# Weight sums over five groups, a pass's feature sums in the next pass, first weights a unit sooner

## The chip, the core and the metric

The kernel runs on one core of a Trainium2 chip, in one launch. The metric is the device time of an execution in microseconds. The five engines of the core run programs of their own and meet at semaphores: TensorE (PE) multiplies, VectorE (DVE) and ScalarE (ACT) work element by element, GpSimd (POOL) and SyncE (SP) here mostly issue transfers (DMAs). In the code `wait_ge` is a wait on a semaphore, `then_inc` counts one up, and `alone` is an empty instruction that carries the waits before it.

## What is computed

One layer of a hybrid encoder, in float32, for 2048 prompt rows and 64 sample rows with caches (2112 rows, model width 1024). Cut to its frame:

```python
q, k, v, z, xbc, dt, u, vc = split_cols(x @ w_in, IN_SIZES)
o_a = band_attention(q, k, v, table)
o_b = mamba_mixer(z, silu(causal_dwconv(xbc)), dt, ...)      # 4 taps
o_c = chunk_mlp(gelu(u), gelu(vc), ...)
x = layer_norm(ALPHA * x + concat(norms) @ w_out)
up = causal_dwconv(x @ ffn_w_in)                             # 3 taps, 2 x 2816 features
gate, val = split_cols(up, (2816, 2816))
x = layer_norm(ALPHA * x + (silu(gate) * val) @ ffn_w_out)
```

Each float32 product is made of three matmuls of halves (high x high, high x low, low x high), so every operand is split into a high part (a copy on ScalarE) and a low part (a subtraction on VectorE). Both projections of the feed-forward part are made with a scheme of seven products for 2 x 2 blocks in place of eight (Strassen's, in Winograd's form), which needs sums and differences of blocks of the weights and of the features.

## The kernel before

Seven stages run one after another: project_rows, project_features, attention, ssd_and_gmlp, mix_out, ffn_up, ffn_down. Within a stage each engine's program has its order written out; what runs when follows from these orders and the semaphores. The change touches project_features, ffn_up and the first waits of ffn_down.

**project_features** (`pf_`) makes queries, keys and xbc with features on partitions. Rows come in groups of 304 (g = 0 to 5, and a last one of 288), 13 units of 24 matmuls each: six of queries and keys, then seven of xbc (the last group takes xbc first). A unit's result lies in one of eight PSUM banks. For xbc unit j, ScalarE copies the bank to `cin` (L792, L790), VectorE makes the four taps into `conv` (L876 to L894), ScalarE applies silu (L779 to L782), SP stores it to xbc_t (L658); `cin`, `conv` and `conv_out` have two buffers each. Beside this VectorE makes, for the down-projection, four sums of blocks of ffn_w_out for each of 11 blocks kk (`sum_weights`, L841 to L848): SP loads 1 MB to `fdw_raw` (one buffer), VectorE sums into `fdw_sum` (one buffer), SP stores it to fd_w_sum and only then loads the next block. The sums come behind xbc units 1, 3, 5 of groups 1, 2 and 4, and behind unit 0 of groups 3 and 5. GpSimd, which loads rows for the groups, then waits for all 11 stores before it loads the attention's bias, queries and keys (L721 to L735).

**ffn_up** (`fu_`) runs three passes q over pairs of row blocks (352 rows each), in each 22 units j, one for each tile of 128 gate and 128 value features. A unit is seven products of 12 matmuls, in the order 1, 2, 6, 5, 7, 3, 4; ScalarE and VectorE combine them as c11 (L2933), c22 (L2951), c12 (L2959) and c21, and TensorE starts product 4 when c22 is taken out of its bank. Then come three taps, silu and the product h = silu(gate) * val (`products_h`, L2857, L2859). Each pair of units gives sums of h for the down-projection (`half_sums`): behind an even unit one difference (L2870), behind an odd one three sums (L2877, L2878, L2881), made between the gate's taps and c22 of the unit after. In the first pass VectorE also sums and splits the weights (L2812 to L2831), which are stored and loaded again by later passes. Values of h lie in `val0`, `val1` or an even tile's own buffer, and go to fd_h_val, fd_h_mix and fd_h_sum. At each turn to the next pass VectorE makes differences of the new features (`differences`, L2614 to L2631) in the last two units. The tensors `xb` are free during a pass, and `half_sum` and the even tiles' first buffers lie over them.

In the third pass the first weights of the down-projection come in too: SP issues four loads of 512 KB (`load_fd_w`, L2529) behind its part of unit 1, and ScalarE and VectorE split two of the pieces in unit 1 (L2775, L2886), between p5's copy and c22, and two in unit 20:

```python
if isinstance(j, int) and j == 1 and q + 1 == NQ:
    sp.wait_ge(x_lo_done, 7 * NQ)
    for piece in range(4):
        load_fd_w(piece)
```

**ffn_down** waits for all stores of h, sums and differences, and multiplies.

## Time and profile before

| what | value |
|---|---|
| time, 3 runs | median 2656.88 us, 2654.92 to 2657.43 |
| the profiled execution's own time | 2656.61 us |
| its span | 2654.8 us |
| PE busy | 2502.1 us (94%) |
| DVE busy | 1799.4 us (68%) |
| ACT busy | 1122.4 us (42%) |
| POOL busy | 199.0 us (7%) |
| moved by DMA | 528.55 MB, mean 199 GB/s |

How the rows are read. Times are microseconds from the span's start. A row of busy times by stretch has: the stretch, its length, then for PE, PEld (PE's weight loads), DVE, ACT and POOL the busy time with the count of instructions, then the granted clock of TensorE as a share of full speed, the mean busy share of the 16 DMA engines, and the GB/s that they moved. A row of a timeline has: start, duration, engine, line, operation, what it writes <- what it reads, the shapes, xcount, and in square brackets how long the engine was idle before it and what ended that; SPq is SP's queue of issues. A row of waits has: who waited <- for whom: us in total, times, longest. A landing row has the time from issue to landing, least/median/most. Matmuls overlap, so one of 0.33 us starts every 0.16.

### The profile page before, as it was taken

Reading aid. Unit: us, or ns where it says so; the run is one execution under the profiler, and the core shown is the slowest. Engines: PE = TensorE matmul, PEld = TensorE weight load, DVE = VectorE, ACT = ScalarE, POOL = GpSimd, SP = SyncE. Lnnn points to the kernel's source line nnn. Section 1 sums busy time; section 2 is a strip of 40 time slices with the busy share of each in tenths; the row PEclk is TensorE's granted clock in tenths of the full one; section 3 lists DMA queues with packets and bytes.
Section 4 is the critical chain, followed back from the end, with each engine's and each line's share of the span. In section 5 each row is a group of like instructions: output and inputs, shape, how many; then the busy total and the mean of one; then the engine's idle time right before and its main releaser. Section 6 shows DMA issues by size and latency. Waiting matters only on the chain. (4 is left out here: it accounts for less than half of the span.)

```text
span 2654.8 us, 45838 instructions
## 1 busy us (share of the span) xinstructions
PE 2502.1 (94%) x14723; PEld 2305.4 (87%) x14723; DVE 1799.4 (68%) x3398; ACT 1122.4 (42%) x2112; POOL 199.0 (7%) x271
## 2 busy tenths in 40 slices
PE   6999988997999989997999989999799999999998
PEld 5888888997999978887999979999799997888786
DVE  5433445565777777778999986667777775355787
ACT  4454412224665552325555554444455453222231
POOL 0001100010101850110000000000000000000000
PEclk9999999998999989998999999999999999999999
DMA  6446545466644654647877779888678867575564
GB/s 206 147 141 204 170 155 182 161 217 160 154 109 124 215 185 152 213 154 252 268 242 248 250 234 297 258 253 261 209 259 257 265 197 207 137 215 140 163 168 137
DMA packets 459877, 528.55 MB, mean 199 GB/s; under 512 B 67690, under 2 KB 381324, under 8 KB 458338
## 3 DMA queue, kind: packets, MB, share of 16 engines
q1 hardware_dynamic: 439356, 464.21, 56.5%
q0 software_dynamic: 19408, 62.38, 7.3%
q8 instruction: 66, 1.08, 0.2%
q10 hardware_dynamic: 998, 0.48, 0.1%
q14 instruction: 49, 0.40, 0.0%
HBM read 342.66 MB, written 187.20 MB: 200 GB/s over the span
## 5 line engine op out<-in xcount | busy, mean ns | idle before, releaser
L2994 PE MATMUL fu_banks<-mo_fu_x_hi,mo_fu_w 128*128 128x354 f32 (+1 forms) x1848 | 609.1, 330 | 58.2 <-DVE fu_c L2951 40.3
L2996 PE MATMUL fu_banks<-mo_fu_x_hi,mo_fu_w 128*128 128x354 f32 (+1 forms) x1848 | 605.6, 328 | 0.0
L2995 PE MATMUL fu_banks<-fu_x_lo_rest,mo_fu_w 128*128 128x354 f32 (+1 forms) x1584 | 518.9, 328 | 0.0
L2994 PEld LDWEIGHTS fu_banks<-mo_fu_x_hi,mo_fu_w 128*128 128x128 f32 x1848 | 353.1, 191 | 69.3 <-issue 27.7
L2996 PEld LDWEIGHTS fu_banks<-mo_fu_x_hi,mo_fu_w 128*128 128x128 f32 x1848 | 353.0, 191 | 0.0
L2995 PEld LDWEIGHTS fu_banks<-fu_x_lo_rest,mo_fu_w 128*128 128x128 f32 x1584 | 302.3, 191 | 0.0
L3302 DVE TENSOR_TENSOR fu_fd_h_a<-fu_fd_h_raw,fu_fd_h_hi 128x768 fp32r<-128x768 f32 x108 | 95.7, 890 | 156.1 <-ACT fu_fd_h_hi L3257 155.8
L3257 ACT CAST fu_fd_h_hi<-fu_fd_h_raw 128x768 fp32r<-128x768 f32 (+1 forms) x116 | 88.1, 761 | 267.5 <-DMA fu_fd_h_raw<-fd_h_sum 106.3
L127 PE MATMUL pr_ps_y<-pr_w_hi,pr_xt_hi 128*128 128x512 f32 (+3 forms) x408 | 148.5, 364 | 4.7 <-DVE pr_xt_lo L404 4.7
L128 PE MATMUL pr_ps_y<-pr_w_lo,pr_xt_hi 128*128 128x512 f32 (+3 forms) x408 | 147.5, 362 | 0.0
L129 PE MATMUL pr_ps_y<-pr_w_hi,pr_xt_lo 128*128 128x512 f32 (+3 forms) x408 | 146.9, 360 | 0.0
L2673 ACT ACTIVATE fu_gate<-fu_c,fu_vecs 128x352 f32<-128x352 f32 (+1 forms) x132 | 90.1, 682 | 73.4 <-DVE fu_c L2933 63.0
L2846 DVE SCALAR_TENSOR_TENSOR fu_gate<-fu_c,fu_vecs,fu_gate 128x352 f32<-128x352 f32 (+1 forms) x132 | 76.9, 583 | 58.1 <-ACT fu_gate L2673 58.1
L1441 PE MATMUL at_ps_o<-pf_at_v,at_pt 128*128 (+2 forms) x900 | 111.7, 269 | 0.0
L127 PE MATMUL mo_ps_y<-sg_mo_w_hi,sg_mo_mt_hi 128*128 128x512 f32 (+1 forms) x272 | 108.2, 398 | 3.4 <-PEq L1490 3.4
L1441 PEld LDWEIGHTS at_ps_o<-pf_at_v,at_pt 128*128 128x128 f32 (+1 forms) x900 | 107.9, 191 | 1.1
L128 PE MATMUL mo_ps_y<-sg_mo_w_lo,sg_mo_mt_hi 128*128 128x512 f32 (+1 forms) x272 | 106.7, 392 | 0.0
L129 PE MATMUL mo_ps_y<-sg_mo_w_hi,sg_mo_mt_lo 128*128 128x512 f32 (+1 forms) x272 | 106.6, 392 | 0.0
L127 PE MATMUL fu_banks<-fu_fd_wa,fu_fd_h_hi 128*128 128x512 f32 x256 | 101.6, 397 | 3.4 <-DVE fu_fd_h_a L3302 2.5
L2823 DVE TENSOR_TENSOR mo_fu_w<-fu_w_raw,mo_fu_w 128x1024 fp32r<-128x1024 f32 x65 | 79.5, 1223 | 32.7 <-ACT mo_fu_w L2646 32.7
L129 PE MATMUL fu_banks<-fu_fd_wa,fu_fd_h_a 128*128 128x512 f32 x256 | 100.9, 394 | 0.0
L128 PE MATMUL fu_banks<-fu_fd_wa,fu_fd_h_hi 128*128 128x512 f32 x256 | 100.9, 394 | 0.0
(462 smaller groups left out, 6001.0 us busy)
## 6 DMA issues: line engine op xcount, KB each, us to landing
mo_fu_w<-fu_w_split SPq DMA_DIRECT2D x176, 512.0 KB, 4.7
fu_w_split<-mo_fu_w SPq DMA_DIRECT2D x44, 1024.0 KB, 4.1
fu_w_raw<-ffn_w_in SPq DMA_DIRECT2D x87, 512.0 KB, 5.5
fd_h_sum<-fu_half_sum SPq DMA_DIRECT2D x22, 528.0 KB, 6.3
pf_fdw_raw<-ffn_w_out SPq DMA_DIRECT2D x11, 1024.0 KB, 7.1
fd_w_sum<-pf_fdw_sum SPq DMA_DIRECT2D x11, 1024.0 KB, 4.8
fu_w_raw<-ffn_w_in SPq DMA_DIRECT2D x44, 256.0 KB, 5.3
x_rows<-pr_xr SPq DMA_DIRECT2D x16, 512.0 KB, 2.9
```

The source lines that it names most:

```text
L127: pe.matmul(out, lhs_hi, rhs_hi, start=first, stop=False)
L128: pe.matmul(out, lhs_hi, rhs_lo, start=False, stop=False)
L129: return pe.matmul(out, lhs_lo, rhs_hi, start=False, stop=last)
L1441: last = pe.matmul(ps_o[:b.nq, par, 0:HD], pt[:w, par, k, :b.nq], vals, start=(k == 0), stop=(k == b.nb - 1))
L2673: act.activation(out, src[:, 0:n], ACT.Identity, bias=one(vecs[:, 3, :], mt), scale=one(vecs[:, 0, :], mt)).then_inc(tap0_done, 1)
L2823: dve.tensor_tensor(w_lo[:, p, W_A11:W_A12 + 1], w_raw[:, p, 0].rearrange("p (a k) c -> p a k c", a=2), w_hi[:, p, W_A11:W_A12 + 1].bitcas ...
L2846: dve.scalar_tensor_tensor(out=out, in0=src[:, 1:1 + n], scalar=one(vecs[:, 1, :], mt), in1=out, op0=ALU.mult, op1=ALU.add).then_inc(tap1_ ...
L2994: pe.matmul(out, wh, xh, start=first and k == 0, stop=False, skip_group_check=True)
L2995: pe.matmul(out, wh, xl, start=False, stop=False, skip_group_check=True)
L2996: last = pe.matmul(out, wl, xh, start=False, stop=k == KH - 1, skip_group_check=True)
L3257: act.copy(h_hi[:, n % RING, 0:raw.shape[1], 0:raw.shape[2]], raw).then_inc(h_hi_done, 1)
L3302: dve.tensor_tensor(low, raw, high.bitcast(F32), ALU.subtract).then_inc(h_lo_done, 1)
```

## The change

Three parts. **Weight sums:** `fdw_raw` holds two blocks; SP issues the first two loads; from then on ScalarE issues the store of a block's sums and the load of the block two further on, behind the silu of the xbc unit after the one that the sums follow. The sums now follow xbc units 1, 4 of groups 0, 2 and 3, units 0, 2, 4 of group 1, and units 0, 2 of group 4. Three empty instructions go, and the loop over groups is written out. **Feature sums:** in the first pass tiles 0 to 19 get no sums (`is_late`). Even and odd tiles both use `val1`, and SP stores them to fd_h_mix. In the second pass SP loads a pair of these tiles back (`load_late`, in the even unit), VectorE makes the four sums in the odd unit (`late_sums`, behind `half_sums`), SP stores them (`store_late`, at that unit's end). `late_raw` and `late_sum` lie over `xb`, so the third pass's differences wait for all late stores; the second pass's no longer wait for sums and differences of the first. **First weights:** the four loads are issued behind SP's part of unit 0 of the third pass.

```diff
--- before.py
+++ after.py
@@ -523,17 +523,13 @@
         ps_y = m.ps("ps_y", [P, 8, 512])
         assert m.here() <= HEAD_AT
-        fdw_raw, fdw_sum = m.over("fdw_raw", raw_at, [P, 2, D]), m.over("fdw_sum", raw_at + 8 * D, [P, 4, 512])
+        fdw_raw, fdw_sum = m.over("fdw_raw", raw_at, [P, 2, 2, D]), m.over("fdw_sum", raw_at + 16 * D, [P, 4, 512])
+        assert 24 * D <= 16 * W
         d["fd_w_sum"] = nc.dram_tensor("fd_w_sum", (KF // 2, P, 4 * 512), F32, kind="Internal").ap()
-        fdw_loaded, fdw_done, fdw_stored = m.sem("fdw_loaded"), m.sem("fdw_done"), m.sem("fdw_stored")
-
-        def fdw_at(g, p, i, j):
-
-            if isinstance(g, int):
-                return {1: 0, 3: 1, 5: 2}.get(j) if g == 1 else None
-            if p:
-                return 4 * i + 2 if j == 0 else None
-            return {1: 4 * i - 1, 3: 4 * i, 5: 4 * i + 1}.get(j)
+        fdw_loaded, fdw_done, fdw_stored = [m.sem("fdw_loaded0"), m.sem("fdw_loaded1")], m.sem("fdw_done"), m.sem("fdw_stored")
+
+
+        FDW = {(0, 1): 0, (0, 4): 1, (1, 0): 2, (1, 2): 3, (1, 4): 4, (2, 1): 5, (2, 4): 6, (3, 1): 7, (3, 4): 8, (4, 0): 9, (4, 2): 10}
         w_loaded = [m.sem(f"w_loaded{k}") for k in range(4)]
         w_hi_done, w_lo_done = m.sem("w_hi_done"), m.sem("w_lo_done")
...
@@ -614,6 +610,10 @@
         def xbc_count(g, j):
             return (NXBC + 1 - j % 2) // 2 * g + j // 2
+
+        def load_fdw(eng, kk):
+            rows = d["ffn_w_out"].rearrange("(k e p) c -> k p e c", e=2, p=P)[kk]
+            eng.dma_start(fdw_raw[:, kk % 2], rows).then_inc(fdw_loaded[kk % 2], 16)
         with nc.Block() as block:
             @block.sync
@@ -625,20 +625,9 @@
                     sp.dma_start(w_raw[:, k % 4, 0:2 * AW], d["w_in"][rows, 0:2 * AW]).then_inc(w_loaded[k % 4], 16)
                     sp.dma_start(w_raw[:, k % 4, 2 * AW:], d["w_in"][rows, X0:X0 + XBC]).then_inc(w_loaded[k % 4], 16)
-                def load_fdw(kk):
-                    pair = slice(kk, kk + 1) if isinstance(kk, int) else bass.ds(kk, 1)
-                    rows = d["ffn_w_out"].rearrange("(k e p) c -> k p e c", e=2, p=P)[pair]
-                    sp.dma_start(fdw_raw[:], rows.rearrange("a p e c -> p (a e) c")).then_inc(fdw_loaded, 16)
-
-                def sums_of(kk):
-
-                    sp.wait_ge(fdw_done, 4 * kk + 4)
-                    alone(sp)
-                    pair = slice(kk, kk + 1) if isinstance(kk, int) else bass.ds(kk, 1)
-                    sp.dma_start(d["fd_w_sum"][pair].rearrange("a p c -> p (a c)"), fdw_sum[:].rearrange("p s c -> p (s c)")).then_inc(fdw_stored, 16)
-
                 sp.wait_ge(w_lo_done, KD - 1)
-                load_fdw(0)
+                for kk in range(2):
+                    load_fdw(sp, kk)
                 def step(g, p, i):
                     n = width(g)
...
-                            sums_of(kk)
-                            if not (p if not isinstance(g, int) else kk == 2):
-                                load_fdw(kk + 1)
-                        if not isinstance(g, int) and p == 0 and j == 0:
-                            load_fdw(4 * i - 1)
                     if tail(g):
                         store_qk(range(AHEAD))
                         sp.wait_ge(states_done, 2)
@@ -781,6 +763,15 @@
                         else:
                             act.activation(conv_out[:, j % 2, :n], conv[:, j % 2, :n], ACT.Silu).then_inc(silu_done, 1)
+                    def behind(j):
+
+                        if (g, j - 1) in FDW:
+                            kk = FDW[g, j - 1]
+                            act.wait_ge(fdw_done, 4 * kk + 4)
+                            act.dma_start(d["fd_w_sum"][kk], fdw_sum[:].rearrange("p s c -> p (s c)")).then_inc(fdw_stored, 16)
+                            if kk + 2 < KF // 2:
+                                load_fdw(act, kk + 2)
+
                     for j in range(NXBC):
                         wait_if(act, conv_done, NXBC * g + j - (1 if j != 0 else 0) if j != 1 else NXBC * g)
                         act.wait_ge(y_done, at_unit(g, 1, j))
@@ -792,7 +783,9 @@
                             act.copy(cin[:, j % 2, 3:3 + n], y).then_inc(evac_done, 1)
                         if j >= 1:
                             silu(j - 1)
+                            behind(j - 1)
                     silu(NXBC - 1)
+                    behind(NXBC - 1)
                     if tail(g):
                         act.wait_ge(ncum_done, 2)
                         act.activation(ecum[:], ncum[:], ACT.Exp, scale=-1.0)
@@ -834,17 +827,14 @@
                 def sum_weights(kk):
-                    b11, b12, b21, b22 = (fdw_raw[:, e, c:c + 512] for e in range(2) for c in (0, 512))
-                    dve.wait_ge(fdw_loaded, 16 * kk + 16)
+                    b11, b12, b21, b22 = (fdw_raw[:, kk % 2, e, c:c + 512] for e in range(2) for c in (0, 512))
+                    dve.wait_ge(fdw_loaded[kk % 2], 16 * (kk // 2 + 1))
                     wait_if(dve, fdw_stored, 16 * kk)
-                    alone(dve)
                     dve.tensor_tensor(fdw_sum[:, 0], b12, b11, ALU.subtract).then_inc(fdw_done, 1)
                     dve.tensor_tensor(fdw_sum[:, 2], b22, b12, ALU.subtract).then_inc(fdw_done, 1)
                     dve.wait_ge(fdw_done, 4 * kk + 1)
-                    alone(dve)
                     dve.tensor_tensor(fdw_sum[:, 1], b22, fdw_sum[:, 0], ALU.subtract).then_inc(fdw_done, 1)
                     dve.wait_ge(fdw_done, 4 * kk + 3)
-                    alone(dve)
                     dve.tensor_tensor(fdw_sum[:, 3], fdw_sum[:, 1], b21, ALU.subtract).then_inc(fdw_done, 1)
                 dve.wait_ge(vec_done, 1)
...
-                            sum_weights(kk)
+                        if (g, j) in FDW:
+                            sum_weights(FDW[g, j])
                     if tail(g):
                         dve.wait_ge(cum_done, 1)
                         dve.tensor_scalar(ncum[:], ps_y[:, 6, 0:NC_ * HEADS].rearrange("p (t h) -> p t h", h=HEADS), -1.0, None,
...
@@ -2326,7 +2315,9 @@
         block_at = [head_at + 4 * KH * WX * slot for slot in range(7)]
         half_sum = m.over("half_sum", block_at[X_T4], [P, 3, 354])
-        even_first = m.over("even_first", block_at[X_T2], [P, 354]), m.over("diff_first", block_at[X_T2] + 1440, [P, 354])
+        late_raw, late_sum = m.over("late_raw", block_at[X_T2], [P, 4, 352]), m.over("late_sum", block_at[X_T3], [P, 4, 352])
+
+        LATE = KF - 2
...
@@ -2409,12 +2401,12 @@
                 return (q + 1, j + n - KF) if q + 1 < NQ else None
             return (q, j + n)
-        def evens(q, j):
-
-            return even_first if q == 0 and not (isinstance(j, int) and j >= KF - 2) else even_later
+        def is_late(q, j):
+            return q == 0 and not (isinstance(j, int) and j >= LATE)
         def second(q, j, p):
-            return val1 if p else evens(q, j)[0]
+
+            return val1 if p or is_late(q, j) else evens[0]
         def raws(q, j, p):
...
@@ -2511,8 +2503,28 @@
                     alone(sp)
                     sp.dma_start(flat(h_val[:, one_tile(j), cols]), val0[:, :n]).then_inc(h_stored[0], 16)
+                def load_late(j):
+
+                    pair = slice(j, j + 2) if isinstance(j, int) else bass.ds(j, 2)
+                    if not isinstance(j, int):
+                        sp.wait_ge(late_done, 2 * j)
+                    sp.wait_ge(h_stored[0], 16 * LATE)
+                    sp.wait_ge(h_stored[1], 16 * LATE)
+                    alone(sp)
+                    sp.dma_start(late_raw[:, 0:2], h_val[:, pair, 0:352]).then_inc(late_loaded, 16)
+                    sp.dma_start(late_raw[:, 2:4], h_mix[:, pair, 0:352]).then_inc(late_loaded, 16)
+
+                def store_late(j):
+
+                    sp.wait_ge(late_done, 2 * j + 2)
+                    alone(sp)
+                    sp.dma_start(h_sum[:, :, one_tile(j), 0:352].rearrange("p s a c -> p (s a) c"), late_sum[:, 0:3]).then_inc(late_stored, 16)
+                    sp.dma_start(flat(h_mix[:, one_tile(j - 1), 0:352]), late_sum[:, 3]).then_inc(late_stored, 16)
...
@@ -2573,6 +2585,11 @@
                             store_h(*before(q, j), 1 - p)
                         if i == (4 if q else 3) and not is_first(q, j):
                             store_sums(*before(q, j), 1 - p)
+                        if q == 1 and not (isinstance(j, int) and j >= LATE):
+                            if i == 1 and p == 0:
+                                load_late(j)
+                            if i == 6 and p:
+                                store_late(j)
                         if i == 3 and last:
                             sp.wait_ge(mm_done, 7 * (NU - 1) + 3)
...
@@ -2584,7 +2601,7 @@
                     if isinstance(j, int) and j == 1 and q + 1 < NQ:
                         sp.wait_ge(x_lo_done, 7 * (q + 1))
                         load_x(q + 1)
-                    if isinstance(j, int) and j == 1 and q + 1 == NQ:
+                    if isinstance(j, int) and j == 0 and q + 1 == NQ:
                         sp.wait_ge(x_lo_done, 7 * NQ)
...
@@ -2609,6 +2626,8 @@
                     eng.wait_ge(xb_loaded[1], loaded_x(q)[0])
                     eng.wait_ge(rest_loaded, loaded_x(q)[1])
                     eng.wait_ge(xb_zeroed, 2 if q == NQ - 1 else 1)
+                    if q == NQ - 1:
+                        eng.wait_ge(late_stored, 16 * LATE)
                     if q:
...
@@ -2619,15 +2638,12 @@
                 def t2_step():
                     eng.wait_ge(t_done, 4 * q + 2)
-                    if q == 1:
-
-                        eng.wait_ge(diff_stored, 16 * (KF // 2 - 1))
                     eng.tensor_tensor(t2, b22, t1, ALU.subtract).then_inc(t_done, 1)
                 def t4_step():
                     eng.wait_ge(t_done, 4 * q + 3)
-                    if q:
-                        eng.wait_ge(sums_stored, 16 * (KF // 2 * q - 1))
+                    if q == NQ - 1:
+                        eng.wait_ge(sums_stored, 16 * (KF // 2))
                     eng.tensor_tensor(t4, b21, t2, ALU.subtract).then_inc(t_done, 1)
                 return t3_step, t1_step, t2_step, t4_step
...
@@ -2742,11 +2759,14 @@
                     if turn:
                         split_x_hi(q + 1, 3)
                     act.wait_ge(add_done, 3 * u + 2)
-                    if p:
-                        wait_if(act, h_stored[1], 8 * u - 8)
-                        wait_if(act, sums_done, 2 * u - 3)
+                    v = u - LATE
+                    if is_late(q, j):
+                        wait_if(act, h_stored[1], 16 * u)
+                    elif p:
+                        act.wait_ge(h_stored[1], 16 * LATE + 8 * v - 8)
+                        wait_if(act, sums_done, 2 * v - 3)
                     else:
-                        wait_if(act, sums_done, 2 * u - 2)
+                        wait_if(act, sums_done, 2 * v - 2)
                         if q == NQ - 1:
                             wait_if(act, rest_stored, 8 * j)
                     if q == NQ - 1:
...
@@ -2879,6 +2902,22 @@
                     dve.wait_ge(sums_done, 2 * u + 1)
                     alone(dve)
                     dve.tensor_tensor(s4, val0[:, :n], s2, ALU.subtract).then_inc(sums_done, 1)
+
+                def late_sums(j):
+
+                    a11, a12, a21, a22 = (late_raw[:, i] for i in range(4))
+                    s1, s2, s4, s3 = (late_sum[:, i] for i in range(4))
+                    dve.wait_ge(late_loaded, 16 * j + 16)
+                    wait_if(dve, late_stored, 16 * j - 16)
+                    alone(dve)
+                    dve.tensor_tensor(s3, a11, a21, ALU.subtract).then_inc(late_done, 1)
+                    dve.tensor_tensor(s1, a21, a22, ALU.add).then_inc(late_done, 1)
+                    dve.wait_ge(late_done, 2 * j - 1)
+                    alone(dve)
+                    dve.tensor_tensor(s2, a22, s3, ALU.subtract).then_inc(late_done, 1)
+                    dve.wait_ge(late_done, 2 * j + 1)
+                    alone(dve)
+                    dve.tensor_tensor(s4, a12, s2, ALU.subtract).then_inc(late_done, 1)
                 def fd_w_lo(piece):
                     high, low, raw = fd_w_piece(piece)
@@ -2941,6 +2980,8 @@
                         split_lo(*nxt, 1 - p, 1)
                     if not is_first(q, j):
                         half_sums(*before(q, j), 1 - p)
+                    if q == 1 and p and not (isinstance(j, int) and j >= LATE):
+                        late_sums(j)
                     for piece in fd_w_here(q, j):
                         fd_w_lo(piece)
...
```

## Rows read from the trace of the kernel before

**Rows 1.** Busy times by stretch: project_features, then pairs and passes of ffn_up.

```profile
334.00:377.33 43.33, 43.16 (x311) 42.91 (x309) 16.88 (x40) 9.12 (x20) 4.21 (x4) 1.00 0.34 107
377.33:435.00 57.67, 48.61 (x312) 47.87 (x313) 35.12 (x86) 14.88 (x28) 0.91 (x1) 0.88 0.53 183
435.00:629.00 194.00, 178.07 (x1257) 176.66 (x1255) 111.50 (x274) 45.22 (x113) 14.93 (x23) 0.96 0.57 185
1257.46:1288.68 31.22, 29.27 (x169) 28.83 (x169) 28.28 (x47) 16.37 (x26) 0.00 (x0) 0.95 0.89 283
1319.11:1349.54 30.43, 27.84 (x168) 27.27 (x169) 28.19 (x47) 16.37 (x26) 0.00 (x0) 1.00 0.78 248
1575.79:1850.04 274.25, 273.64 (x1681) 273.00 (x1681) 192.43 (x343) 127.61 (x220) 0.00 (x0) 1.00 0.85 267
1600.00:1628.90 28.90, 28.90 (x178) 28.64 (x177) 20.28 (x37) 13.07 (x23) 0.00 (x0) 1.00 1.04 324
```

**Rows 2.** Timeline of TensorE in project_features, its two longest waits.

```profile
398.24 0.62 PE L127 MATMUL pf_ps_y<-pr_pf_xs,pr_pf_w 128*128 128x304 f32 x1 [6.66 <-ACT pf_cin L792]
...
606.83 0.61 PE L127 MATMUL pf_ps_y<-pr_pf_xs,pr_pf_w 128*128 128x288 f32 x1 [7.30 <-ACT pf_cin L790]
```

**Rows 3.** Timeline of VectorE in project_features; landing of the stores of pf_fdw_sum.

```profile
374.01 0.16 DVE L876 COPY pf_cin<-pf_halo 128x3 f32<-128x3 f32 x1
...
439.91 0.69 DVE L841 TENSOR_TENSOR pf_fdw_sum<-pf_fdw_raw 128x512 f32<-128x512 f32 x1 [6.06 <-DMA pf_fdw_raw<-ffn_w_out]
...
442.51 0.16 DVE L876 COPY pf_cin<-pf_halo 128x3 f32<-128x3 f32 x1
...
444.77 0.16 DVE L876 COPY pf_cin<-pf_halo 128x3 f32<-128x3 f32 x1
...
DMA to landing us min/median/max: 3.9/4.8/7.3
```

**Rows 4.** Timeline in project_features, one instruction of ScalarE, one of GpSimd.

```profile
605.90 0.39 ACT L779 ACTIVATE pf_conv_out<-pf_conv 128x224 f32<-128x224 f32 x1 [9.97 <-DMA xbc_t<-pf_conv_out]
...
581.32 0.83 POOL L722 DMA_DIRECT2D pf_bias<-pf_bias_rows  x1 [95.08 <-DMA fd_w_sum<-pf_fdw_sum]
```

**Rows 5.** Waits of TensorE in the first pass; timeline of VectorE there.

```profile
PE fu_banks L2994 <- DVE fu_c L2951: 23.4, 17, 2.1
...
1332.59 0.52 DVE L2870 TENSOR_TENSOR fu_diff_first<-fu_val,fu_even_first 128x352 f32<-128x352 f32 x1
...
1333.02 0.52 DVE L2951 TENSOR_TENSOR fu_c<-fu_part,fu_banks 128x354 f32<-128x354 f32 x1
...
1347.39 0.52 DVE L2877 TENSOR_TENSOR fu_half_sum<-fu_even_first,fu_val 128x352 f32<-128x352 f32 x1
...
1348.89 0.52 DVE L2951 TENSOR_TENSOR fu_c<-fu_part,fu_banks 128x354 f32<-128x354 f32 x1
```

**Rows 6.** Timeline of VectorE at the turn to the second pass.

```profile
1547.61 1.63 DVE L2631 TENSOR_TENSOR mo_fu_xb<-mo_fu_xb 128x1416 f32<-128x1416 f32 x1 [3.34 <-DMA fd_h_sum<-fu_half_sum]
```

**Rows 7.** Timelines in the later passes of ffn_up.

```profile
1697.36 0.52 DVE L2951 TENSOR_TENSOR fu_c<-fu_part,fu_banks 128x354 f32<-128x354 f32 x1 [0.65 <-PE fu_banks L2996]
...
1834.02 2.26 SPq L2545 DMA_DIRECT2D mo_fu_w<-fu_w_split  x2
...
1840.26 1.63 DVE L2614 TENSOR_TENSOR mo_fu_xb<-mo_fu_xb 128x1424 f32<-128x1424 f32 x1
...
2169.03 2.35 DVE L2886 TENSOR_TENSOR fu_fd_wa<-fu_fd_wa_raw,fu_fd_wa 128x1024 fp32r<-128x1024 f32 x2
...
2171.87 0.43 PE L2994 MATMUL fu_banks<-mo_fu_x_hi,mo_fu_w 128*128 128x356 f32 x1 [0.98 <-DVE fu_c L2951]
```

**Rows 8.** Timelines at the third pass's second unit, by start.

```profile
1899.11 2.38 SPq L2529 DMA_DIRECT2D fu_fd_wa_raw<-ffn_w_out  x4
...
1905.08 1.04 ACT L2775 CAST fu_fd_wa<-fu_fd_wa_raw 128x1024 fp32r<-128x1024 f32 x1 [9.82 <-DMA fu_fd_wa_raw<-ffn_w_out]
...
1909.24 0.66 PE L2994 MATMUL fu_banks<-mo_fu_x_hi,mo_fu_w 128*128 128x356 f32 x1 [10.59 <-DVE fu_c L2951]
```

50 lines of the change are left out of this document (27 added, 23 removed).

## The prediction

> **What bounds the kernel now.** I read the page first: TensorE is busy for 94% of the span and VectorE for 68%, averages over stages with different limits. So the busy times by stretch came second, with a stretch for each stage that the change touches; then the waits of TensorE in these stretches; then the timeline of VectorE, ScalarE and the DMA queues around each wait.
>
> In project_features a group of 13 units takes 43.33 us where TensorE never waits. The next 13 took 57.67 us with 48.61 busy and a granted clock of 0.88, and the rest of the stage 194.00 us [rows 1]. The largest waits are 6.66 us and, in the last group, 7.30 us, both for ScalarE's copies out of PSUM [rows 2]. Behind the first stands a chain: VectorE waits 6.06 us for a weight block that one buffer holds [rows 3], ScalarE waits for VectorE's convolution, TensorE for ScalarE. Behind the second, ScalarE waits 9.97 us for a store of xbc_t to land, in the stretch in which GpSimd's queue moves the attention's first tiles; GpSimd had stood 95.08 us for the last weight sums before it began [rows 4].
>
> In ffn_up's first pass a pair of units takes 30.43 us with VectorE busy for 28.19, or 31.1 to 31.2 at clock 0.95. The second pass needs 274.25 us for 20 units with TensorE busy for all but 0.6 and VectorE for 70% [rows 1]: 13.68 us a unit, 27.4 a pair. In the first pass TensorE waits for VectorE's c22 17 times, 23.4 us [rows 5]: VectorE is the bound there, TensorE in the second. At the third pass's second unit TensorE stands 10.59 us [rows 8].
>
> **Part 1, the sums of weights.** The work is the same: 11 blocks, each 2.60 us on VectorE (439.91 to 442.51), against 2.26 us for one convolution (442.51 to 444.77) [rows 3]. What goes is the wait for the block, since two are held and each is asked for two sums ahead. What comes is a wait for the sums' store before fdw_sum is written again. The store is issued by ScalarE behind the next silu and lands in 3.9 to 7.3 us, median 4.8 [rows 3]. Sums two units apart wait for it, three apart hardly.
>
> ScalarE now issues a store and a load at each sum. Nearest price: four loads issued by SP took 2.38 us, 0.6 each [rows 8], so at most 1.2 a sum. Queued behind them is the next copy into cin, and behind that VectorE and TensorE. Silu, two issues and copy need about 2.1 us, less than a convolution. I charge nothing to VectorE and count 0.8 us on each copy behind a sum. SP's queue loses both transfers, and xbc_t's stores no longer stand behind them.
>
> After group 0 the two sums there delay VectorE by 5 to 8 us. Group 1's convolutions began at 374.01 [rows 3], though the matmuls of its first xbc unit were through by 334 + 7 x 3.33 = 357.3: VectorE works through queries and keys first, which wait for their stores, and the bias rows travel at the time. These stores do not all shift, so part of the delay is absorbed. I take C = 377 (bounds 374, nothing arrives, and 380). With sums behind j = 0, 2 and 4, the copies that TensorE needs at 377.33 plus 3.33 for each unit stand at C+3.2, C+8.8, C+10.3, C+19.4 and C+21.5: C, one convolution more for each, 2.60 for a sum, and 2.3 to 3.5 for the store not yet landed. TensorE stands 2.9, 2.3, 0, 3.9 and 0 us: 9.1, against the 9.06 idle (57.67 less 48.61) of now. So these 13 units gain nothing: between 3 better at C = 374 and 3 worse at 380, the slower clock with them a little more.
>
> From group 2 on VectorE keeps up: it is busy 111.50 us of the 194 [rows 1], 28 for each group of 13 units, sums in them; even with 8 us of waits for stores that is 36, under 43.33. I expect no wait of TensorE. The rest of the stage becomes 3 x 43.33 for three groups and 41.8 for the last (288 of 304 columns, and the decay sums): 172 instead of 194 [rows 1], so 22 less. This takes the 7.30 us with it: the last sums are stored in group 4, some 50 us sooner, and the bias and the first keys travel during group 5's copies, whose banks are wanted again four units or 13.3 us later. Bounds: 27 if C stays, 10 if the tail still stands its 7.3 with its slow restart and C is late.
>
> The Trainium skill (DMA: Bandwidth & Descriptors, Issuing engines are not separate DMA queues) says that DMAs of ScalarE and SP run on the same 16 engines and that a second issuer saves issue time only. By it, landings would stay as they are, which the sum above supposes.
>
> **Part 2, the first pass's sums.** Removed from each pair: the difference (1332.59 to 1333.02, 0.43 us) and three sums (1347.39 to 1348.89, 1.50) [rows 5]. VectorE is the bound, so a pair becomes 30.43 - 1.93 = 28.5, still over TensorE's 27.4. Ten pairs: 19.3 us. Five of the ten now run about 0.7 longer at clock 0.95; with waits of 0.6 instead of 1.95 I expect clock 1.00: 3.4 more, 22.7. Floor: 27.4 a pair would give 33; ceiling: only 19. val1 now serves even tiles too, so ScalarE must wait for h_mix's store; it is issued some 5 us before (products_h, then c11, one sum and the gate's taps lie between). A store of 1 MB lands in 4.8 [rows 3]; this one has 176 KB: nothing. If it took 7, 2 us a unit would come back.
>
> At the turn to the second pass VectorE waited 3.34 us for the last store of half_sum [rows 6]; that buffer lies idle now. Gain 3.3.
>
> The second pass gets 4 more operations in each odd unit. They stand ahead of c22 and cost 1.94 us (0.43 each, and one dependence). There VectorE had come 0.65 us too soon [rows 7], so c22 moves by 1.29. How much it bears is shown at the last but one unit: 2.35 us of fd_w_lo put ahead of c22 cost TensorE 0.98 [rows 7]; slack 1.3 to 1.4. So 0 to 0.2 an odd unit: 1 us in all, bound 6 if the even unit's slack is not the odd one's. SP gets two loads and two stores a pair; ahead of load_w and of the h stores they take 1.2 us each time, behind a unit of slack.
>
> At unit 20 the differences for the third pass overwrite late_sum, and wait for the last late store. SP issues it behind load_w, from 1836.3 on (1834.02 + 2.26), two transfers, landed some 6 us later (the 4.8 of rows 3 and the issue of two), at 1842.3; VectorE wants to begin at 1840.26 [rows 7]. 2 us late, and c22, c12 and the splits of x behind it: 2 us (0 to 5).
>
> Transfers: a pair gains 704 KB of loads and as much of stores, 1.44 MB in 27.4 us, 53 GB/s on top of 267 [rows 1]: 320. The stretch at 1600 shows 324 for 28.9 us with TensorE never idle. Just hidden; load_w has a unit of slack.
>
> **Part 3, the down-projection's first weights.** The four loads go out behind unit 0's last load_w instead of unit 1's, one unit or 13.7 us sooner: 1885.4 instead of 1899.11. The first landed in 6.0 (1899.11 to 1905.08) [rows 8]: now at 1891.4, the second by 1893. ScalarE comes for them at 1895.26 (1905.08 - 9.82). SP's next load_raw waits 2.4 us behind them, two units ahead of its use. Left are two casts and two subtractions before c22, which cost 0.98 at the other such place [rows 7]; casts come first here, so 0.65. Gain 9.9, and 1.3 for the clock: the first matmul behind took 0.66 instead of 0.43 [rows 7, 8] (bounds 0 and 6, since 9.06 idle in rows 1 went with 5.3 more lost).
>
> **Sum.** 22 + 22.7 + 3.3 + 11.2 - 1 - 2 = 56.2 us. The profiled execution took 2656.61 around a span of 2654.8; less 56.2 it is 2600.4, and the median shown is 0.3 higher: 2600.7.
>
> **Rivals.**
> A: group 0's sums push group 1 behind the bias rows' traffic, C is 385 or the store lands in 7 us, so groups 1 to 3 stay late, and the tail still waits for xbc_t: part 1 gives 8. For it: the 16.7 us that the convolutions of group 1 are late already now. Against: VectorE's load is under TensorE's from group 2 on. 2615. Chance 0.20.
> B: the late sums reach TensorE in every odd unit by the whole 1.2 us, with the clock dips that rows 1 show for waits of 2 us: 12 to 15 back. For it: slack measured in an even unit only. 2613. Chance 0.15.
> C: the first pass falls to TensorE's own pace, 27.4 a pair: 10 more. Against: 28.5 counted on VectorE. 2590. Chance 0.10.
> D, slower: the second pass becomes bound by transfers. It would have to move no more than 267 GB/s in the mean: 8.77 MB at 267 is 32.8 us a pair, 5.4 x 10 = 54 back, and at 250 it is slower by 20: 2677. Against: 324 over 28.9 us. The Trainium skill (DMA: Bandwidth & Descriptors, Where 436 GB/s comes from) puts the HBM side at about 358 GB/s for a core; by that 320 still fits, with little left. Chance 0.03.
> E: the stalls have another cause than the waits I named, and nothing moves: 2657. Chance 0.02.
> The forecast has 0.50: its own range is 2592 to 2609. The whole range, 2586 to 2622, takes in A to C and leaves out D, E and the ends. A measurement here tells about 0.2%, 5 us, from no change. Faster 0.95, same 0.02, slower 0.03.
>
> **What would show it.** In the profile after: no wait of VectorE for weight blocks in project_features, one or two of 2 to 3.5 us for their store, and TensorE's waits in that stage about 9 us, all near group 2's start; pairs of 28.5 us in the first pass; 13.7 a unit and some 320 GB/s in the second; one wait of 2 us of VectorE at its unit 20; about 0.65 us instead of 10.59 at the third pass's second unit. Waits behind group 2, a second pass over 277 us for the same 20 units, or ScalarE waiting for h_mix would make it wrong.

## The result and the profile after

The changed kernel takes 2615.37 us (median of 4 runs, 2614.35 to 2618.04) against 2655.9 for the kernel before on the same chip (4 runs, 2654.37 to 2657.43): ratio 0.9849, 95% interval 0.9832 to 0.9866. That is 40.5 us faster where 56.2 were forecast. The time lies in the whole range (2586 to 2622) and outside the forecast's own (2592 to 2609). The profiled execution took 2615.82 us around a span of 2614.0, 40.8 less than the 2654.8 of before.

Four matmuls cut both traces into stages: project_features' first (287.84 before, 287.46 after), the attention's first (634.14 and 620.34), ffn_up's first (1207.36 and 1188.18) and ffn_down's first (2197.18 and 2156.65). The ledger by stage, in us, with ffn_up cut further:

| part of the span | before | after | measured | forecast |
|---|---|---|---|---|
| project_features to the attention | 346.30 | 332.88 | -13.4 | -22 |
| attention, segment sums, mix | 573.22 | 567.84 | -5.4 | 0 |
| ffn_up's first pass with its turn | 368.43 | 348.14 | -20.3 | -22.7 - 3.3 |
| second pass, 20 units | 274.25 | 284.85 | +10.6 | +3 |
| turn to the third pass | 34.67 | 34.67 | 0 | 0 |
| third pass | 287.16 | 275.43 | -11.7 | -11.2 |
| the rest (start, last unit, ffn_down) | 770.8 | 770.2 | -0.6 | 0 |

The ffn_up rows run between the matmuls that follow a c22 (before: 1575.79, 1850.04, 1884.71 and 2171.87, of which [rows 1, 7] show the ends; after: 1536.32, 1821.17, 1855.84 and 2131.27), the first from ffn_up's first matmul.

Busy times by stretch of the kernel after. The first two stretches answer to 334 to 435 and 435 to 629 in [rows 1], the third to the pair there, the fourth to its second pass:

```profile
333.62:444.20 110.58, 92.62 (x620) 90.77 (x619) 60.15 (x142) 23.14 (x48) 5.11 (x5) 0.92 0.57 193
444.20:617.28 173.08, 173.08 (x1257) 172.81 (x1255) 107.03 (x267) 44.31 (x114) 14.77 (x23) 1.00 0.54 176
1298.53:1327.08 28.55, 27.85 (x168) 27.27 (x169) 26.40 (x43) 16.37 (x26) 0.00 (x0) 1.00 0.76 246
1536.32:1821.17 284.85, 277.58 (x1681) 274.42 (x1681) 210.90 (x383) 126.66 (x220) 0.00 (x0) 0.99 0.99 305
```

The last 1257 matmuls of project_features take 173.08 us instead of 194.00, with TensorE never idle and clock 1.00, where 172 was forecast. The two groups ahead of them take 110.58 instead of 101.00: there the gain is given back. The pair of the first pass takes 28.55 (forecast 28.5). In the second pass TensorE is busy for 277.58 us, 3.9 more than the 273.64 of [rows 1], and idle for 7.3 where it was idle for 0.6; the DMA share is 0.99.

TensorE's three largest waits in project_features after, with VectorE's timeline in the same stage and the landing of the stores of pf_fdw_sum:

```profile
350.50 0.41 PE L127 MATMUL pf_ps_y<-pf_xs_slot,pr_pf_w 128*128 128x304 f32 x1 [3.19 <-ACT pf_cin L783]
...
392.77 0.59 PE L127 MATMUL pf_ps_y<-pr_pf_xs,pr_pf_w 128*128 128x304 f32 x1 [8.41 <-ACT pf_cin L783]
...
408.15 0.62 PE L127 MATMUL pf_ps_y<-pr_pf_xs,pr_pf_w 128*128 128x304 f32 x1 [2.99 <-ACT pf_cin L783]
```
```profile
349.44 0.69 DVE L833 TENSOR_TENSOR pf_fdw_sum<-pf_fdw_raw 128x512 f32<-128x512 f32 x1 [6.03 <-DMA fd_w_sum<-pf_fdw_sum]
...
389.36 0.16 DVE L866 COPY pf_cin<-pf_halo 128x3 f32<-128x3 f32 x1
```
```profile
DMA to landing us min/median/max: 3.9/5.0/10.5
```

Before its second sum of group 0 VectorE waits 6.03 us: the store of the first landed in 10.5 us, over the 7.3 that was the most before [rows 3]. Group 1's convolutions begin at 389.36 instead of 374.01 [rows 3]. TensorE pays for it already inside group 1 (3.19 us) and then at group 2 (8.41 and 2.99). Behind 409 TensorE has no wait of 0.9 us or more in this stage: the 7.30 us of [rows 2] are gone, and VectorE waits for no block load any more.

GpSimd's queue stood beside that store (timeline, and the row of DMA issues with its time to landing):

```profile
336.76 1.11 POOL L697 DMA_DIRECT2D pf_bias_rows<-rel_ext  x1 [5.97 <-PE pf_ps_y L129]
354.42 1.10 POOL L697 DMA_DIRECT2D pf_bias_rows<-rel_ext  x1 [16.55 <-PE pf_ps_y L129]
```
```profile
pf_bias_rows<-rel_ext POOLq DMA_DIRECT2D x1, 640.0 KB, 26.3
```

At ffn_up's first pass one wait is new, at the third unit. TensorE's timeline, with the regular wait of a later pair under it; ScalarE's; and SP's queue of issues:

```profile
1244.72 0.42 PE L3035 MATMUL fu_banks<-mo_fu_x_hi,mo_fu_w 128*128 128x354 f32 x1 [2.45 <-DVE mo_fu_w L2851]
...
1298.53 0.42 PE L3035 MATMUL fu_banks<-mo_fu_x_hi,mo_fu_w 128*128 128x354 f32 x1 [0.49 <-DVE fu_c L2992]
```
```profile
1241.95 0.68 ACT L2689 ACTIVATE fu_val<-fu_c,fu_vecs 128x352 f32<-128x352 f32 x1 [6.01 <-DMA fd_h_mix<-fu_val]
```
```profile
1223.40 5.38 SPq L2467 DMA_DIRECT2D mo_fu_xb<-x1t  x4
1229.22 5.00 SPq L2450 DMA_DIRECT2D fu_w_raw<-ffn_w_in  x2
1234.57 3.01 SPq L2499 DMA_DIRECT2D fd_h_mix<-fu_val  x1
```

ScalarE waits 6.01 us for the store of h_mix from the one value buffer. That store's issue alone took 3.01 us (others: 0.34 to 0.37, one 0.51), behind two loads of weights (5.00) and the four loads of the next x (5.38). The two pairs from 1236.17 to 1298.53 take 62.36 instead of 2 x 28.55: 5.3 lost, once.

In the second pass, TensorE's two waits, ScalarE's and VectorE's that lie behind them, and three of ScalarE's copies of c11's part (one a unit):

```profile
1573.35 0.43 PE L3035 MATMUL fu_banks<-mo_fu_x_hi,mo_fu_w 128*128 128x354 f32 x1 [3.61 <-ACT fu_part L2726]
...
1818.33 0.43 PE L3035 MATMUL fu_banks<-mo_fu_x_hi,mo_fu_w 128*128 128x354 f32 x1 [3.02 <-ACT fu_part L2745]
```
```profile
1572.30 0.64 ACT L2689 ACTIVATE fu_val<-fu_banks,fu_vecs 128x352 f32<-128x352 f32 x1 [7.01 <-DMA fd_h_val<-fu_val]
...
1600.55 0.46 ACT L2726 COPY fu_part<-fu_banks 128x354 f32<-128x354 f32 x1 [1.21 <-PE fu_banks L3037]
...
1614.48 0.46 ACT L2726 COPY fu_part<-fu_banks 128x354 f32<-128x354 f32 x1 [0.96 <-PE fu_banks L3037]
...
1628.13 0.46 ACT L2726 COPY fu_part<-fu_banks 128x354 f32<-128x354 f32 x1 [1.21 <-PE fu_banks L3037]
```
```profile
1811.38 1.64 DVE L2633 TENSOR_TENSOR mo_fu_xb<-mo_fu_xb 128x1424 f32<-128x1424 f32 x1 [2.81 <-DMA fd_h_mix<-fu_late_sum]
```

The copies stand 13.93 and 13.65 us apart in turn; before it was 13.65 each time. So the late sums ahead of c22 cost 0.28 us in every odd unit, 2.8 in all; it does not show as idle time, since matmuls overlap. What it is shows at one matmul behind c22, which starts 0.33 us after the one ahead of it instead of 0.16 and takes 0.42 instead of 0.33:

```profile
1609.96 0.32 PE L3037 MATMUL fu_banks<-mo_fu_x_hi,mo_fu_w 128*128 128x354 f32 x1
1610.29 0.42 PE L3035 MATMUL fu_banks<-mo_fu_x_hi,mo_fu_w 128*128 128x354 f32 x1
```

One wait of 3.61 us stands near the pass's start, behind ScalarE's 7.01 for h_val's store; one of 3.02 at its unit 20, behind VectorE's 2.81 for the last late store. These are 9.4 of the 10.6 us. Behind the first wait the granted clock falls to 0.86 in a stretch of 10 us, which is 1.4 us lost if all of it delays the matmuls, and so about the rest of 1.2; from 1590 to 1818 it is 1.00:

```profile
1575.00:1585.00 10.00, 10.00 (x55) 10.00 (x55) 7.80 (x16) 3.87 (x7) 0.00 (x0) 0.86 1.08 369
```

At the third pass's second unit, TensorE in place of the 10.59 us of [rows 8]:

```profile
1870.23 0.44 PE L3035 MATMUL fu_banks<-mo_fu_x_hi,mo_fu_w 128*128 128x356 f32 x1 [0.45 <-DVE fu_c L2992]
```

### The profile page after: what moved, and what is told of

Same layout as the page of the kernel before. It is cut to its first block and busy times, and to the rows that moved or that the text cites. A ratio compares the mean times of both kernels' runs of the same rounds, so it can differ in the third digit from the quotient of the medians.

```text
span 2614.0 us, 45349 instructions
## 1 busy us (share of the span) xinstructions
PE 2488.4 (95%) x14723; PEld 2290.0 (88%) x14723; DVE 1799.6 (69%) x3398; ACT 1118.0 (43%) x2109; POOL 199.2 (8%) x271
## 3 DMA queue, kind: packets, MB, share of 16 engines
q1 hardware_dynamic: 442204, 452.25, 56.2%
## 5 line engine op out<-in xcount | busy, mean ns | idle before, releaser
L3035 PE MATMUL fu_banks<-mo_fu_x_hi,mo_fu_w 128*128 128x354 f32 (+1 forms) x1848 | 607.0, 328 | 40.5 <-DVE fu_c L2992 12.9
L3035 PEld LDWEIGHTS fu_banks<-mo_fu_x_hi,mo_fu_w 128*128 128x128 f32 x1848 | 350.7, 190 | 54.2 <-ACT fu_part L2745 13.4
```

What stands on the lines that cost most here:

```text
L3035: pe.matmul(out, wh, xh, start=first and k == 0, stop=False, skip_group_check=True)
```

## The experiments

Every kernel was profiled and timed beside the kernel before, in five rounds (the one with more traffic in three). The stage between the attention's first matmul and ffn_up's first took 566 to 582 us in these profiles though no edit touches it, and single times of one kernel spread over up to 22 us. So effects of a few us are read from stage times in the profiles, and the ratios stand beside them. Stage times have a spread of their own, which kernels with the same program of a stage show: project_features takes 329.6 to 334.5 us in the six kernels that have it as after, and 321.7 to 325.8 in the four with the sums a group later; ffn_up takes 968.5 to 971.1 and its second pass 300.5 to 302.8 in the four that have these as after. An effect of 2 us on a stage is hardly more than that, and rests on the single waits named beside it. "Second pass" is here 21 units, from the first c22 matmul of the pass (1536.32 after) to the one with a wait of 1.1 to 1.7 us at the turn (1836.79).

| kernel | median | ratio to before (95%) | project_features | middle | ffn_up | second pass |
|---|---|---|---|---|---|---|
| before | | | 346.30 | 573.22 | 989.82 | 289.88 |
| after | 2615.37 | 0.9849 (0.9832-0.9866) | 332.88 | 567.84 | 968.47 | 300.47 |
| e1 part 1 only | 2642.66 | 0.995 (0.9931-0.9969) | 331.27 | 568.27 | 989.43 | 289.63 |
| e2 parts 2, 3 only | 2633.33 | 0.9916 (0.99-0.9932) | 344.84 | 566.87 | 970.19 | 302.10 |
| e3 sums later | 2608.82 | 0.9832 (0.981-0.9854) | 321.92 | 566.07 | 968.52 | 300.55 |
| e4 two buffers | 2623.69 | 0.9868 (0.9849-0.9888) | 332.47 | 578.42 | 966.20 | 301.08 |
| e5 loads behind | 2616.95 | 0.9856 (0.9832-0.9881) | 334.51 | 570.96 | 966.54 | 298.73 |
| e7 x in halves | 2612.36 | 0.9849 (0.9824-0.9873) | 329.63 | 576.59 | 962.01 | 297.71 |
| e8 swapped, behind | 2617.9 | 0.9857 (0.9832-0.9882) | 333.70 | 577.75 | 964.75 | 296.42 |
| e9 all five | 2603.58 | 0.9821 (0.9799-0.9842) | 321.71 | 573.90 | 957.31 | 294.73 |
| e10 late sums behind | 2607.01 | 0.9814 (0.9797-0.9831) | 325.44 | 571.36 | 961.67 | 298.94 |
| e11 more traffic | 2625.25 | 0.9877 (0.9853-0.9901) | 334.38 | 581.77 | 972.74 | 304.67 |
| e12 bias later | 2616.6 | 0.9857 (0.9839-0.9876) | 326.91 | 571.76 | 971.12 | 302.84 |
| e13 late sums split | 2599.14 | 0.9766 (0.9748-0.9785) | 325.80 | 576.66 | 954.99 | 292.40 |

**Part 1 alone.** The kernel before with the diff's hunks in project_features.

```diff
 kernel before, and of the diff only the hunks from
-        fdw_raw, fdw_sum = m.over("fdw_raw", raw_at, [P, 2, D]), ...
...
-                        kk = fdw_at(g, p, i, j)
+                        if (g, j) in FDW:
```

> The kernel before with part 1 alone (the sums of weights spread over five groups, in project_features). In the trace after the stage from the first matmul of project_features to the attention's first took 332.88 us instead of 346.30, and what lies between there and ffn_up's first matmul 567.84 instead of 573.22. Theory: both belong to part 1 (its last sums are stored earlier, so fewer transfers stand in the way of the attention's and the segment sums' first loads): 18.8 us faster, about 2637. Rival: only the stage itself is part 1's and the 5.4 us behind it vary by themselves or belong to the rest: 13.4 faster, about 2642.

The ratio gives 13 us (0.995 of 2654.8), and the stage falls by 15.0 us; ffn_up stays at 989.4. The middle is 568.27, but it is 566.87 in the next run too, which has project_features as before. So the 5.4 us of the middle do not need part 1, and are put down to its variation: the rival holds.

**Parts 2 and 3 alone.** The kernel before with the diff's hunks in ffn_up and ffn_down.

```diff
 kernel before, and of the diff only the hunks from
-    fd.update({... ("diff_stored", "sums_stored", "rest_stored")})
+    fd.update({... ("diff_stored", "sums_stored", "rest_stored", "late_stored")})
...
+                sp.wait_ge(fd["late_stored"], 16 * late)
```

> The kernel before with parts 2 and 3 alone (everything in ffn_up and what ffn_down waits for). Theory: the parts do not touch each other; ffn_up gives 21.4 us as in the trace after (989.82 to 968.47 us), about 2634.5, with VectorE's c22 no longer the bound of the first pass and two waits of 3.6 and 3.0 us of TensorE at the second pass's units 2 and 20. Rival: the first pass's one-off wait of ScalarE for the store of h_mix (6.01 us) comes from traffic that depends on what ran before, and is not there: 26 us faster, about 2630.

22 us by the ratio (0.9916), 19.6 by the stage of ffn_up, with waits of 4.65 and 2.47 us where after has 3.61 and 3.02. The one-off wait of the first pass is there too (2.43 us on TensorE), so it does not depend on what ran before. The stage times of the two add up: 15.0 + 19.6 against 13.4 + 21.4 in after.

**Sums of weights a group later.**

```diff
-        FDW = {(0, 1): 0, (0, 4): 1, (1, 0): 2, (1, 2): 3, (1, 4): 4, (2, 1): 5, ... (4, 0): 9, (4, 2): 10}
+        FDW = {(1, 1): 0, (1, 4): 1, (2, 0): 2, (2, 2): 3, (2, 4): 4, (3, 1): 5, ... (5, 0): 9, (5, 2): 10}
```

> The kernel after with every sum of weights one group later (groups 1 to 5 instead of 0 to 4). Theory: the sums of group 0 are what made group 1 late. Their stores and loads stand in the transfers of the bias rows (the store of the first took 10.5 us, and VectorE waited 6.03 us for it), so without them group 1's convolutions begin near 374 again instead of 389, and TensorE's waits of 3.2, 8.4 and 3.0 us in groups 1 and 2 shrink to some 3 us in all: 12 to 20 us faster than after, about 2600. Rival: group 1 is late because of its own stores of queries and keys (4 waits of 3.9 to 11.4 us) whatever group 0 does, and the sums that come into groups 1 and 5 cost what leaves group 0: within 3 us of after, about 2615.

The stage takes 321.92 us, 11.0 less than after; over all profiles with either order the means differ by 9.2 (the expected 12 to 20 was too high). VectorE's timeline and TensorE's:

```profile
373.86 0.16 DVE L866 COPY pf_cin<-pf_halo 128x3 f32<-128x3 f32 x1
```
```profile
385.56 0.41 PE L127 MATMUL pf_ps_y<-pr_pf_xs,pr_pf_w 128*128 128x304 f32 x1 [1.33 <-ACT pf_cin L783]
...
437.30 0.41 PE L127 MATMUL pf_ps_y<-pf_xs_slot,pr_pf_w 128*128 128x304 f32 x1 [3.33 <-ACT pf_cin L783]
...
595.20 0.33 PE L970 MATMUL pf_ps_y<-ident,pf_halo 128*21 128x128 f32 x1 [3.21 <-DVE pf_conv L884]
```

Group 1's convolutions begin at 373.86, as in the kernel before. So group 0's two sums are the whole of the 15.3 us of delay. Three smaller waits remain. The last stands at the tail, near the sums that are now in group 5; that they cause it is argued and not shown. It is 3.01 to 6.40 us in the four kernels with this order.

**A second value buffer.** Even tiles of the first pass go to even_first again, with a semaphore of its own.

```diff
-            return val1 if p or is_late(q, j) else evens[0]
+            return val1 if p else even_first if is_late(q, j) else evens[0]
...
-                        wait_if(act, h_stored[1], 16 * u)
+                        if p:
+                            wait_if(act, h_stored[1], 8 * u - 8)
+                        else:
+                            wait_if(act, even_stored, 8 * u)
```

> The kernel after with the even tiles of the first pass written to a buffer of their own again (even_first, with a semaphore of its own for its store), so that ScalarE does not wait for the store of the tile just before. Theory: the wait of 6.01 us at the first pass's second unit goes, and with it TensorE's 2.45 and 1.94 us and their clock: 5 us faster than after, about 2610. Rival: h_val's store stands behind h_mix's in the same queue and lands as late, and val0 is wanted by ScalarE next: 1 us faster or nothing, about 2615.

The result lies between theory and rival. The two pairs at the one-off wait take 59.50 us (1246.39 to 1305.89) instead of 62.36; ScalarE then waits 3.78 us for h_val, the store behind it. Of 5.3 us the buffer gives back 2.9; ffn_up is 2.3 shorter. The median is over that of after, since the middle was 10.6 us longer in this profile. One of its five runs took 8265 us, for a reason that is not known, and the ratio leaves it out.

**Late loads behind the stores.**

```diff
-                            if i == 1 and p == 0:
+                            if i == 3 and p == 0:
                                 load_late(j)
```

> The kernel after with the two loads for the late sums issued by SP behind the stores of the unit before, instead of ahead of them. Judged by the second pass's 20 units (284.85 us after, 274.25 before), since the stages between project_features and ffn_up vary by 12 us from run to run. Theory: TensorE's 3.61 us at the second pass's unit 2 are partly the 1.4 us that SP spends on these two issues ahead of h_val's store, for which ScalarE waits: 1.4 of wait and some clock, the 20 units in about 283. Rival: the store is late by the burst of transfers alone (eight loads of x just ahead), and the order on SP changes nothing: 285.

The 20 units take 283.09 us, 1.8 less (theory: 283). TensorE's wait is 2.11 instead of 3.61. In the next kernel but one, with the same order, it is 2.45; the six kernels with the loads ahead and the x in one piece show 3.60 to 5.08. So the shorter wait is this edit's.

**The next x in halves.**

```diff
-                    if isinstance(j, int) and j == 1 and q + 1 < NQ:
+                    if isinstance(j, int) and j < 2 and q + 1 < NQ:
                         sp.wait_ge(x_lo_done, 7 * (q + 1))
-                        load_x(q + 1)
+                        load_x(q + 1, (j,))
```

> The kernel after with the loads of the next pass's x issued half behind unit 0 and half behind unit 1, instead of all behind unit 1. Theory: both one-off waits of ScalarE (6.01 us for h_mix at the first pass's unit 2, 7.01 us for h_val at the second pass's unit 2) come from this burst: SP's four issues took 5.38 us, the two weight loads behind 5.00 and h_mix's store 3.01, where they otherwise take 1.1 and 0.36. In halves the pair of units 2 and 3 of the first pass falls from 33.8 to under 31 us and the second pass's 20 units from 284.9 to under 283; ffn_up 3 to 6 us shorter than 968.5. Rival: the burst only moves, and the halves delay the stores of two units instead of one: no shorter, or longer by 2.

ffn_up is 6.5 us shorter (962.01). ScalarE's wait for h_mix, with SP's issues ahead of it:

```profile
1244.60 0.68 ACT L2691 ACTIVATE fu_val<-fu_c,fu_vecs 128x352 f32<-128x352 f32 x1 [2.51 <-DMA fd_h_mix<-fu_val]
```
```profile
1229.54 2.38 SPq L2467 DMA_DIRECT2D mo_fu_xb<-x1t  x2
1232.37 4.79 SPq L2450 DMA_DIRECT2D fu_w_raw<-ffn_w_in  x2
1237.50 2.80 SPq L2501 DMA_DIRECT2D fd_h_mix<-fu_val  x1
```

The two pairs take 58.84 us (1242.31 to 1301.15), 1.7 over the regular 57.1, and TensorE's wait at the burst of the second pass is 0.88, with a new one of 1.14 for c22 behind it. One edit in the order of SP's queue shrinks both one-off waits, so both come from this burst. It is not gone: h_mix's store still needs 2.80 us to be issued.

**Late blocks swapped,** on top of the loads behind the stores.

```diff
-        late_raw, late_sum = m.over("late_raw", block_at[X_T2], ...), m.over("late_sum", block_at[X_T3], ...)
+        late_raw, late_sum = m.over("late_raw", block_at[X_T3], ...), m.over("late_sum", block_at[X_T2], ...)
...
-                    if q == NQ - 1:
-                        eng.wait_ge(late_stored, 16 * LATE)
...
                 def t2_step():
...
+                    if q == NQ - 1:
+                        eng.wait_ge(late_stored, 16 * LATE)
```

> The edit of the run before last (loads behind) and besides late_raw and late_sum in each other's blocks: the differences for the third pass overwrite late_raw first, which nothing in flight reads, and late_sum two steps later, and the wait for the last late store moves to that step. Theory: TensorE's 3.02 us at the second pass's unit 20 are this wait (VectorE's 2.81 us), and the store has long landed two steps later: 3 us of wait and 1 of clock, ffn_up 4 us shorter than with the loads behind alone. Rival: VectorE's load of work in this unit (two differences of 1.64 us each ahead of c12) is what is late, and the wait hides inside it: 0 to 1 us.

The wait for the late store, 2.79 us with the loads behind alone, is gone, and only the regular 0.61 behind it is left. The 20 units take 280.79 us instead of 283.09, and ffn_up is 1.8 shorter. The place was right; the expected 4 us was too much, also because the wait at the burst was 2.45 here instead of 2.11.

**All five.**

> The kernel after with all five edits together: sums of weights a group later, a second value buffer in the first pass, late loads behind the stores, x in halves, late blocks swapped. Theory: the gains add, since each has a place of its own: project_features 11 us (as measured in that run's stage), first pass 5, second pass 8: 24 us faster than after, about 2591, and faster than before by 64. Rival: the edits in ffn_up remove the same waits twice (the second buffer and the halves both serve h_mix's store), and the second pass stays at its transfers' pace: 15 faster, about 2600.

project_features gives 11.2 us, ffn_up 11.2: 22.3 together, near the theory's 24. The whole time shows less: the median of 2603.58 is 11.8 below after's and nearer the rival's 2600, and the middle, which no edit touches, was 6.1 us longer in this profile. The two pairs at the one-off wait take 57.10 (1231.24 to 1288.34), so the burst is harmless once both the buffer and the halves are there. Neither was enough alone. Busy times of its second pass:

```profile
1526.01:1805.11 279.10, 276.31 (x1680) 272.87 (x1681) 210.62 (x383) 126.32 (x220) 0.00 (x0) 1.00 1.01 314
```

The intervals against before (0.9799 to 0.9842, after 0.9832 to 0.9866) still touch.

**Late operations behind c12,** on all five.

```diff
-                    if q == 1 and p and not (isinstance(j, int) and j >= LATE):
-                        late_sums(j)
...
                     taps(q, j, 2, second(q, j, p)[:, :n], c22)
+                    if q == 1 and p and not (isinstance(j, int) and j >= LATE):
+                        late_sums(j)
```

> The run before it (all five edits) and besides the four late operations of VectorE behind c12 and the taps of c22 in the odd unit, instead of ahead of c22. In the trace after, the copies of c11's part come 13.65 and 13.93 us apart in turn in the second pass (13.65 always in the kernel before). Theory: the 0.27 us of each second interval are the late operations ahead of c22; behind it they fall into VectorE's idle time, the interval becomes 13.65 throughout, and the second pass's 20 units take 2.7 us less than the 279.1 of all five. Rival: they delay the operations of the next unit as much, or the interval is the transfers' doing (the DMA engines are at 1.00), and 279 stays.

The rival holds, and more: a pair takes 28.11 us instead of 27.58, TensorE waiting in each even unit. ffn_up is 4.4 us longer than with all five; the ratios (0.9814 and 0.9821) do not tell the two apart.

```profile
1613.38 0.42 PE L3045 MATMUL fu_banks<-mo_fu_x_hi,mo_fu_w 128*128 128x354 f32 x1 [0.54 <-DVE fu_c L3000]
...
1641.49 0.42 PE L3045 MATMUL fu_banks<-mo_fu_x_hi,mo_fu_w 128*128 128x354 f32 x1 [0.53 <-DVE fu_c L3000]
```

**More traffic.**

```diff
+                            if i == 5 and not isinstance(j, int):
+                                sp.dma_start(scratch[one_tile(j)]..., h_val[:, 0:2, 0:352]).then_inc(copied, 16)
```

> The kernel after with one more transfer from DRAM to DRAM in each unit from 2 to 19 of the second pass, two tiles of h_val (352 KB read and as much written) into an array that nothing reads. It adds work and changes no result. The second pass runs with the DMA engines busy at 1.00 and 305 to 310 GB/s. Theory: this is the edge; nothing more hides, and a unit grows from 13.8 by about the transfer's own share of the engines, 1.5 to 2.5 us: the 20 units take 315 to 330 us instead of 285. Rival: the queues' busy share counts waiting too and there is room up to the 348 to 360 GB/s that single stretches of 10 us show: under 292 us.

The rival holds. Its second pass in the steady part:

```profile
1595.00:1830.00 235.00, 234.97 (x1428) 232.68 (x1427) 174.46 (x320) 107.84 (x187) 0.00 (x0) 0.99 1.04 336
```

336 GB/s instead of 306, a share of 1.04, and TensorE idle for 0.03 us in 235: a pair still takes 27.58 us. What grew is the wait at the burst (5.08 instead of 3.61) and that for the last late store (3.69 instead of 3.02), and the first matmul behind either took 0.66 us instead of 0.43. The second pass is 4.2 us longer with them. Without this traffic the wait at the burst was already 4.65 and 4.70 in two other kernels, so it is not shown that the traffic lengthened it. Single stretches moved more still, with TensorE busy throughout:

```profile
1695.00:1705.00 10.00, 10.00 (x63) 10.00 (x63) 7.61 (x14) 4.81 (x8) 0.00 (x0) 1.00 1.05 384
```

**Bias rows later.**

```diff
                 step(0, 0, 0)
                 step(1, 1, 0)
-                for h in range(0, HEADS, 2):
-                    pool.wait_ge(y_done, NM + 2 * h + 1)
-                    ...
                 with pool.Fori(1, NG // 2 - 1) as i:
...
+                for h in range(0, HEADS, 2):
+                    pool.wait_ge(y_done, 3 * NM + 2 * h + 1)
+                    ...
                 step(NG - 2, 0, NG // 2 - 1)
```

> The kernel after with GpSimd's three transfers of bias rows (640 KB each, in small packets) issued from the fourth group on instead of in group 0 and 1; the sums of weights stay in group 0. Theory: these transfers, 17 to 26 us long each, are what the stores stand in: the first store of sums (10.5 us), xbc_t's (7.8 us of ScalarE's wait) and qk_lo's (11.4, 3.9, 4.7 and 3.9 us of VectorE's waits) land in 2 to 5 us, group 1's convolutions begin before 374 instead of at 389, and TensorE's waits of groups 1 and 2 (17.9 us) go: 12 to 20 us less than the 332.9 us of the stage. Rival: the stores are late because of the loads of x and of weights beside them (1.2 MB and 1 MB), and the bias rows only share the time: under 3 us, with the same waits again in the group to which they move.

Both were half right. In groups 0 and 1 the theory holds: VectorE does not wait for group 0's store of sums, which lands in 4.6 us, group 1's convolutions begin at 368.93, and of TensorE's waits up to group 2 (14.6 us in the three large ones) one of 2.12 is left. But the same waits appear where the bias rows now travel:

```profile
468.48 0.38 PE L127 MATMUL pf_ps_y<-pf_xs_slot,pr_pf_w 128*128 128x304 f32 x1 [2.52 <-DVE pf_qk_lo L852]
...
480.38 0.59 PE L127 MATMUL pf_ps_y<-pr_pf_xs,pr_pf_w 128*128 128x304 f32 x1 [6.77 <-ACT pf_cin L783]
```

The stage is 6.0 us shorter than after (2.7 under the shortest of the six with after's program), less than the 11.0 of moving the sums. The expectation's "small packets" do not fit the trace: the rows travel in packets of 5120 bytes, beside entries of 8 bytes. Why they hold other transfers up stays open.

**Two late operations ahead of c22 and two behind,** on all five.

```diff
                     if q == 1 and p and not (isinstance(j, int) and j >= LATE):
-                        late_sums(j)
+                        late_sums(j, 0)
...
                     taps(q, j, 2, second(q, j, p)[:, :n], c22)
+                    if q == 1 and p and not (isinstance(j, int) and j >= LATE):
+                        late_sums(j, 1)
```

> The kernel with all five edits, and of the four late operations in each odd unit two (0.9 us) stay ahead of c22 and two (1.0 us) go behind c12 and the taps. Theory: each c22 bears a fixed slack. All four ahead cost the odd unit's c22 0.27 us a pair (27.58 against 27.31), all four behind cost the even unit's c22 more (28.10); so the slack is about 1.7 us in the one place and 1.1 us in the other, and two and two fit into both: pairs of 27.31 us, the 20 units in 276 to 277 us instead of 279.1, ffn_up 2.5 us shorter than 957.3. Rival: what VectorE has to do in a pair of units is the bound whatever the place, or the slack of one is the other's: 27.5 or more, 279 stays.

Copies of c11's part by ScalarE, and the busy times of the 20 units:

```profile
1621.47 0.46 ACT L2733 COPY fu_part<-fu_banks 128x354 f32<-128x354 f32 x1 [1.21 <-PE fu_banks L3051]
...
1635.12 0.46 ACT L2733 COPY fu_part<-fu_banks 128x354 f32<-128x354 f32 x1 [0.96 <-PE fu_banks L3051]
...
1648.77 0.46 ACT L2733 COPY fu_part<-fu_banks 128x354 f32<-128x354 f32 x1 [1.21 <-PE fu_banks L3051]
```
```profile
1533.64:1810.41 276.77, 274.43 (x1680) 272.94 (x1680) 210.79 (x383) 127.25 (x220) 0.00 (x0) 1.00 0.98 317
```

13.65 us each time, 276.77 us for the 20 units, ffn_up 2.3 shorter than with all five. The ratio to before is 0.9766 (0.9748 to 0.9785), clear of that of after: this is the fastest version, 61 us under the 2660.18 us of the kernel before in its rounds. By the ratio it is some 15 us better than all five, of which the stage shows 2.3; the rest is not this edit's as far as the profile shows, and has no explanation here.

## Why the prediction was right in direction and 15 us short

**What held.** The main terms stood within about 1 us: the last three groups and the tail of project_features (173.08 against 172), the pair of the first pass (28.55 against 28.5), that pass with its turn once its one-off loss is set aside (20.3 + 5.3 against 26), and the third pass (11.7 against 11.2; the wait is 0.45 where 0.65 was expected). Removing VectorE's work from a pass that VectorE bounds gave it all back, and the clock with it: over eight pairs 30.78 us each became 28.55 in the regular ones, 2.2 less where the work was 1.93.

**What did not.** Two of the three signs that the prediction named against itself came: a second pass of 284.85 us, over 277, and ScalarE waiting for h_mix. The total is inside the whole range in part by luck: 5.4 us came from the middle, which was forecast at 0, and without them the time would be some 2621, next to the end at 2622.

**A reading.** The prediction puts VectorE's wait of 6.06 us behind TensorE's of 6.66 us at 398.24, but it stands at 439.91, after it. The one ahead of it has the same cause, so the chain holds:

```profile
392.31 0.69 DVE L841 TENSOR_TENSOR pf_fdw_sum<-pf_fdw_raw 128x512 f32<-128x512 f32 x1 [6.26 <-DMA pf_fdw_raw<-ffn_w_out]
```

**Group 0's sums, the step that failed most.** The prediction took "C = 377", three us late, since "these stores do not all shift, so part of the delay is absorbed", and counted the idle time of groups 1 and 2 as equal to before. It expected 5 to 8 us of delay from the two sums. All of it arrived, and more: C was 389.36. The sums cost 5.2 us of work and one wait of 6.03 for a store that landed in 10.5 us beside 640 KB of bias rows (in 4.6 with the bias rows elsewhere); nothing of this was absorbed, and VectorE's waits in group 1's queries and keys, 26.6 us, were 3.7 longer than with the sums a group later. TensorE was idle for 18.0 us in groups 1 and 2 (110.58 less 92.62) where 9.1 were counted, part of it in group 1, which the sum had left out. Moving group 0's sums (11.0 us back) and moving the bias rows (group 1 back in time) show both halves of this. This term was 8.6 short. Rival A named this mechanism and its price, 2615; that the time agrees is partly chance. A expected the tail to go on waiting, which it did not, and the other shortfalls lie in ffn_up.

**One value buffer for the first pass.** The prediction let ScalarE wait for h_mix's store and took "nothing", from stores that land in 4.8 us. In the steady units that is right. It did not look at the one unit where SP issues the next x: 5.3 us. This is the second failed step. The second buffer and the halves together remove it.

**Second pass.** "0 to 0.2 an odd unit: 1 us in all" measured 0.28 and 2.8: the slack was taken from an even unit and is a little less in the odd one. "2 us late" at unit 20 measured 2.81 on VectorE and 3.02 on TensorE. The 3.61 us at unit 2 was in no term. It is the burst of x again, now with late loads ahead of h_val's store in the queue; the loads put behind it gave 1.8 back, x in halves more. Rival B is refuted in its size (0.28, not 1.2), rival C by the pair of 28.55, rival D altogether: 305 GB/s hid, and 336 did too. Rival E is refuted by both parts.

The Trainium skill (DMA: Bandwidth & Descriptors, Where 436 GB/s comes from) puts the HBM side at about 358 GB/s for a core. Here that was no ceiling: 336 in the mean still hid, and stretches of 10 us moved 369 in after and 384 with more traffic, TensorE busy throughout. The Trainium skill (DMA: Bandwidth & Descriptors, Issuing engines are not separate DMA queues) says that another issuer saves issue time only; the stores of sums, issued by ScalarE now, land in 5.0 us in the median against 4.8 of SP's [rows 3], which agrees.

**The middle.** Its 5.4 us came unasked and belong to no part: across the profiles it is 566 to 582 us. Most of that lies in the segment sums, 118.11 to 132.02 us from their first matmul to mix_out's. The shortest and the longest, in the profiles of the sums a group later and of more traffic:

```profile
830.23:948.34 118.11, 106.85 (x854) 103.40 (x855) 86.77 (x182) 68.87 (x190) 96.10 (x102) 0.95 0.69 212
844.19:976.21 132.02, 122.25 (x854) 118.54 (x855) 86.42 (x182) 69.00 (x190) 96.41 (x102) 0.82 0.61 189
```

TensorE is idle for 11.3 and 9.8 us, and the other engines are busy for as long in both. What differs is the granted clock, 0.95 and 0.82 in the mean, and with it TensorE's busy time. Why the clock is lower in one run than in the other is not shown.

So the profiled difference of 40.8 us holds some 35 of the change (15.0 and 19.6 by the stages of the parts alone, 13.3 and 22.3 by their ratios). The medians put it at 35.6 to 44.6 us (the ratio's interval), so the 35 lie at its lower end.

Open stays also what causes the wait of 3.3 us at 437.30. Three of the four versions with the sums a group later show it (3.21 to 3.33 us), the fourth 1.25, and after does not.

## What to carry to other kernels

Work put into a stage with room in the mean still needs a look at the one group in which other transfers already stand: the cost was in group 0's store beside the bias rows and in the one unit with the burst of x, not in the averages. When one buffer takes the place of two, search the whole loop for the latest landing of its store, and read the issue times of the queue ahead of it. Where extra operations sit ahead of a critical one, the slack differs by place: here all of them ahead of c22 cost 0.28 us a pair, all behind it 0.80, and half and half nothing.

## What the runs showed of the hardware that was not expected

- An issue on SP is not of fixed price: the store of h_mix took 0.37 us to issue in most units and 3.01 behind the burst of x and weights, and a pair of weight loads 5.00, where most took 1.0 to 1.9.
- The mean busy share of the DMA engines reads 1.00 at 306 GB/s and 1.04 at 336 GB/s with TensorE never waiting, so a share of 1 did not mean that transfers were the bound.
- One transfer of 640 KB of bias rows took 26.3 us (the other two of after 17.0 and 18.0, the three of before 17.0 to 18.7), and a store of 1 MB issued beside it 10.5 instead of some 5.
- The same instructions of the segment sums took 118 us at a mean granted clock of 0.95 and 132 at 0.82, in two profiles of kernels that are alike there.
